# Inverting 16-token diagonal blocks on VectorE, with one doubling stage of two products, in a hybrid retention and gated-delta block

## The reference, cut to what matters

```python
kk = jnp.einsum("bhncd,bhnsd->bhncs", k, k)
lower = jnp.where(strict, beta[..., :, None] * kk * decay, 0.0)
a_mat = jnp.broadcast_to(eye, lower.shape) + lower
sol = lax.linalg.triangular_solve(a_mat, rhs, left_side=True, lower=True, unit_diagonal=True)
...
ret_out = ro * jax.nn.silu(rg)
...
gdn_out = go.reshape(b, t, GDN_W) * jax.nn.silu(gz)
```

## Time and profile before

| | |
|---|---|
| Time, median (lowest to highest) | 2764.13 us (2758.5 to 2767.09) |
| The profiled execution | 2768.09 us, span 2765.9 us |
| Granted TensorE clock | 0.993 |
| PE busy | 98% of the span |
| POOL, DVE, ACT busy | 60%, 53%, 38% |
| The chain that ended last | PE 86%, DVE 7%, issue 3%, POOL 2% |

### The profile page before, as it was taken

How to read it: one execution, slowest core, us unless ns; L and a number is a source line. 1 busy time by engine, 2 the same in 40 slices (tenths; PEclk the granted TensorE clock), 3 DMA queues, 4 the chain that set the end, 5 groups by cost and what they waited for, 6 DMA issues and landing times.

```text
span 2765.9 us, 36134 instructions
## 1 busy us (share of the span) xinstructions
PE 2702.6 (98%) x13344; PEld 2261.7 (82%) x13344; DVE 1462.1 (53%) x2423; ACT 1057.9 (38%) x1831; POOL 1647.1 (60%) x1260
## 2 busy tenths in 40 slices
PE   5899999999999999999999999999999999999998
PEld 4788888888888888888888888888888888888886
DVE  5867667454758475644456445663535553322223
ACT  3533333353334433443344424353333333443332
POOL 3745555576666755665566755576555566665653
PEclk9999999999999999999999999999999999999999
DMA  7334454332333223322232323422222224233242
GB/s 277 115 109 139 151 176 153 126 116 94 111 127 117 96 92 121 112 94 85 89 130 93 103 83 111 143 86 88 88 88 84 88 81 145 92 99 99 92 130 84
DMA packets 98238, 311.56 MB, mean 113 GB/s; under 512 B 11536, under 2 KB 11536, under 8 KB 95888
## 3 DMA queue, kind: packets, MB, share of 16 engines
q1 hardware_dynamic: 67248, 246.85, 27.1%
q10 hardware_dynamic: 30816, 62.40, 6.8%
HBM read 285.09 MB, written 24.12 MB: 112 GB/s over the span
## 4 chain that ended last, share of the span: by engine, by line
PE 86%; DVE 7%; issue 3%; POOL 2%; DMA 1%; ACT 1%; ACTq 0%; SPq 0%; DVEq 0%; POOLq 0%
PE acc L510 25%; PE acc L512 24%; PE acc L511 24%; PE pm L545 6%; PE pm L550 1%; DVE mixing L1242 1%; DVE x L1525 1%; PE pm L672 1%; PE pm L647 1%; DMA mixing<-in_ada_w 1%; POOL w L1693 1%; PE pm L600 1%; PE pm L642 1%; POOL mT L1702 1%; PE pm L657 0%
## 5 line engine op out<-in xcount | busy, mean ns | idle before, releaser
L1693 POOL TENSOR_TENSOR w<-raw,w 128x512 fp32r<-128x512 f32 x832 | 1117.7, 1345 | 938.6 <-ACT w L754 936.3
L754 ACT ACTIVATE w<-raw 128x512 fp32r<-128x512 f32 x832 | 520.9, 627 | 773.6 <-PE acc L512 722.7
L510 PE MATMUL acc<-mT,w 128*128 128x512 f32 x1536 | 623.3, 406 | 8.0 <-DVE mT L1587 3.2
L512 PE MATMUL acc<-mT,w 128*128 128x512 f32 x1536 | 601.9, 392 | 0.0
L511 PE MATMUL acc<-mT,w 128*128 128x512 f32 x1536 | 600.5, 391 | 0.0
L510 PE MATMUL acc<-hid,w 128*128 128x512 f32 x864 | 348.6, 404 | 2.2 <-DVE ffs L1485 1.4
L510 PEld LDWEIGHTS acc<-mT,w 128*128 128x128 f32 x1536 | 290.4, 189 | 67.2 <-issue 5.0
L512 PEld LDWEIGHTS acc<-mT,w 128*128 128x128 f32 x1536 | 289.5, 189 | 62.8
L512 PE MATMUL acc<-hid,w 128*128 128x512 f32 x864 | 337.4, 391 | 0.0
L511 PE MATMUL acc<-hid,w 128*128 128x512 f32 x864 | 336.8, 390 | 0.0
L511 PEld LDWEIGHTS acc<-mT,w 128*128 128x128 f32 x1536 | 290.8, 189 | 54.2 <-issue 1.0
(11 more groups left out here) (234 smaller groups left out, 3649.9 us busy)
## 6 DMA issues: line engine op xcount, KB each, us to landing
raw<-in_w_all SPq DMA_DIRECT2D x416, 512.0 KB, 3.5
ada_late<-in_ada_w SPq DMA_DIRECT2D x32, 512.0 KB, 5.5
xr<-in_xT ACTq DMA_DIRECT2D x48, 256.0 KB, 3.5
mixing<-in_ada_w SPq DMA_DIRECT2D x8, 1024.0 KB, 9.5
proj_kept<-ffs ACTq DMA_DIRECT2D x32, 256.0 KB, 2.1
out<-io ACTq DMA_DIRECT2D x32, 256.0 KB, 2.5
mixed_kept<-mixing ACTq DMA_DIRECT2D x28, 256.0 KB, 2.0
xr<-mixed_kept ACTq DMA_DIRECT2D x28, 256.0 KB, 2.7
```

What stands on the lines that cost most here:

```text
L510: e.matmul(bank, whi, x[:, 0, :], start=first, stop=False)
L512: m = e.matmul(bank, wlo, x[:, 0, :], start=False, stop=last)
L754: e.activation(w2[:, 0, local % HALVES, :], raw[:, tile % NRAW, local % 2 * NT:(local % 2 + 1) * NT], ACT.Copy).then_inc(S["w_hi"], 1)
L1693: e.tensor_tensor(w2[:, 1, local % HALVES, :], raw[:, tile % NRAW, local % 2 * NT:(local % 2 + 1) * NT], w2[:, 0, local % HALVES, :].bitca ...
```

## The change

The blocks that DVE inverts are 16 wide (OCT = 16). Its inversion has 15 steps of a product and a sum on 128x64 elements, in slots 20 to 27, two steps a slot. The running inverse `inv8` lies in the first 64 columns of PSUM bank bE, where it was in `octs`; `part8` and the rows stay in SBUF. There are 4 row buffers (ROWS): four shuffles follow `near`, and each of the first 11 steps ends with the shuffle of the row four further on. The expansion to `U` and the transpose to `T` are at s = 29.

Stage 0 now widens from 16 to 64 with its four products, at slots 32, 34, 36 and 38. After it `U` is updated by DVE, and the top left 64x64 part of each tile is transposed to `T` with three `transpose`s of 32 partitions by 4x32 elements. The last doubling, 64 to 128, is two products only, at slots 40 and 42, and one subtraction. So a unit has six `four`s for the inverse where it had eight. The masks for the stages change with the sizes; POOL's second one goes from s = 34 to 36. Both gate products are issued at s = 16, ahead of `r_state` and `LT` of s = 17.

```diff
-OCT = 8
+OCT = 16
+ROWS = 4
+YSTEPS = 4
...
-        near, inv8, part8 = (oct_cols(i) for i in range(3))
+        near, part8 = oct_cols(0), oct_cols(1)
+        inv8 = bE[:, 0:SUB * OCT].rearrange("p (t j) -> p t j", j=OCT)
 
         def near_row(i):
-            return oct_cols(3 + i)
+            return oct_cols(2 + i % ROWS)
+
+        def block_step(n, i):
+
+            return OSTEPS * n + 1 + ROWS + 2 * i + min(i, OCT - 1 - ROWS)
...
-                st, step = divmod(s - 30, 8)
-                if 0 <= st < STAGES and step == 0:
+                if s in (32, 40):
+                    st = (s - 32) // 8
                     e.wait_ge(S["lvl_mask"], STAGES * n + st + 1)
                     if st == 0:
                         e.wait_ge(S["k_nat"], n + 1)
                         e.wait_ge(S["t_ready"], n + 1)
                     else:
-                        e.wait_ge(S["t_next"], (STAGES - 1) * n + st)
+                        e.wait_ge(S["t_next"], 3 * (n + 1))
                     four(bE, Lm, T).then_inc(S["x_out"], 1)
-                if 0 <= st < STAGES and step == 2:
+                if s in (34, 42):
+                    st = (s - 34) // 8
                     e.wait_ge(S["x_ready"], STAGES * n + st + 1)
                     if st:
-                        e.wait_ge(S["u_turned"], (STAGES - 1) * n + st)
+                        e.wait_ge(S["u_half"], n + 1)
                     else:
                         e.wait_ge(S["u_first"], n + 1)
                         e.wait_ge(S["lt_ready"], n + 1)
                     four(bB, X, U).then_inc(S["y_out"], 1)
-                if 0 <= st < STAGES and step == 4:
-                    e.wait_ge(S["q_ready"], 2 * STAGES * n + 2 * st + 1)
+                if s == 36:
+                    e.wait_ge(S["q_ready"], 2 * n + 1)
                     four(bB, X, Q).then_inc(S["y_out"], 1)
-                if 0 <= st < STAGES and step == 6:
-                    e.wait_ge(S["q_ready"], 2 * STAGES * n + 2 * st + 2)
-                    if st == 0:
-                        e.wait_ge(S["attn_ready"], n + 1)
-                    if st < STAGES - 1:
-                        four(bF, Q, X).then_inc(S["y_out"], 1)
-                    else:
-                        four(bF, X, Q).then_inc(S["y_out"], 1)
+                if s == 38:
+                    e.wait_ge(S["q_ready"], 2 * n + 2)
+                    e.wait_ge(S["attn_ready"], n + 1)
+                    four(bF, X, Q).then_inc(S["y_out"], 1)
...
+                def row_of_block(i):
+
+                    e.stream_shuffle(octs[:, 2 + i % ROWS, :], octs[:, 0, :], [OCT * (q // OCT) + i for q in range(32)]).then_inc(
+                        S["oct_steps"], 1)
...
-                if s == 26:
+                if s == 16:
                     twice_silu(S["tanh_rg"], n, gts[:, 0, :], gts[:, 0, :], pr[:, RG - RK, :], S["y_rg"])
-                if s == 28:
+                if s == 16:
                     twice_silu(S["tanh_gz"], n, gts[:, 1, :], gts[:, 1, :], pr[:, GZ - RK, :], S["y_gz"])
...
-                    for i in range(OCT - 1):
-                        e.stream_shuffle(octs[:, 3 + i, :], octs[:, 0, :], [OCT * (q // OCT) + i for q in range(32)]).then_inc(
-                            S["oct_steps"], 1)
-                for i in {20: (0, 1), 21: (2, 3), 22: (4, 5), 23: (6,)}.get(s, ()):
-                    done = OSTEPS * n + OCT + 2 * i
+                    for i in range(ROWS):
+                        row_of_block(i)
+                for i in (2 * (s - 20), 2 * (s - 20) + 1):
+                    if not (20 <= s < 28 and i < OCT - 1):
+                        continue
                     if n == 0 and i == 0:
                         e.wait_ge(S["eye8_ready"], 1)
+                    if i == 0:
+                        e.wait_ge(S["k_nat"], n + 1)
                     before = inv8 if i else eye8.unsqueeze(1).to_broadcast([P, SUB, OCT])
-                    e.wait_ge(S["oct_steps"], done)
+                    e.wait_ge(S["oct_steps"], block_step(n, i - 1) + 2 if i else block_step(n, 0))
                     e.tensor_tensor(part8, near_row(i), before[:, :, i:i + 1].to_broadcast([P, SUB, OCT]),
                                     ALU.mult).then_inc(S["oct_steps"], 1)
-                    e.wait_ge(S["oct_steps"], done + 1)
+                    e.wait_ge(S["oct_steps"], block_step(n, i) + 1)
                     e.tensor_tensor(inv8, before, part8, ALU.add).then_inc(S["oct_steps"], 1)
-                if s == 25:
+                    if i + ROWS < OCT - 1:
+                        row_of_block(i + ROWS)
+                if s == 29:
                     e.wait_ge(S["oct_steps"], OSTEPS * (n + 1))
                     e.tensor_tensor(by_oct(U), inv8.unsqueeze(2).to_broadcast([P, SUB, P // OCT, OCT]),
                                     lmask[:, 1, :].rearrange("p (b j) -> p b j", j=OCT).unsqueeze(1).to_broadcast(
                                         [P, SUB, P // OCT, OCT]), ALU.mult).then_inc(S["u_first"], 1)
                     e.wait_ge(S["u_first"], n + 1)
                     e.transpose(T, U).then_inc(S["t_ready"], 1)
-                st, step = divmod(s - 30, 8)
-                if 0 <= st < STAGES and step in (2, 4):
-                    e.wait_ge(S["y_out"], 3 * STAGES * n + 3 * st + step // 2)
-                    if st:
-                        e.wait_ge(S["u_turned"], (STAGES - 1) * n + st)
+                if s in (34, 36):
+                    at = (s - 34) // 2
+                    e.wait_ge(S["y_out"], YSTEPS * n + at + 1)
+                    e.wait_ge(S["u_first"], n + 1)
+                    if at == 0:
+                        e.wait_ge(S["mg_kept"], 16 * ((HEADS - 1) * (n // HEADS) + n % HEADS))
                     else:
-                        e.wait_ge(S["u_first"], n + 1)
-                    if st == 0 and step == 2:
-                        e.wait_ge(S["mg_kept"], 16 * ((HEADS - 1) * (n // HEADS) + n % HEADS))
+                        e.wait_ge(S["q_ready"], 2 * n + 1)
                     e.tensor_tensor(Q, U, bB, ALU.subtract).then_inc(S["q_ready"], 1)
-                if 0 <= st < STAGES and step == 6:
-                    e.wait_ge(S["y_out"], 3 * STAGES * n + 3 * st + 3)
-                    if st < STAGES - 1:
-                        if st:
-                            e.wait_ge(S["t_next"], (STAGES - 1) * n + st)
-                        else:
-                            e.wait_ge(S["t_ready"], n + 1)
-                        e.tensor_tensor(T, T, bF, ALU.subtract).then_inc(S["t_next"], 1)
-                        e.wait_ge(S["t_next"], (STAGES - 1) * n + st + 1)
-                        e.transpose(U, T).then_inc(S["u_turned"], 1)
-                    else:
-                        e.wait_ge(S["u_turned"], (STAGES - 1) * (n + 1))
-                        e.tensor_tensor(U, U, bF, ALU.subtract).then_inc(S["u_next"], 1)
+                if s == 38:
+                    e.wait_ge(S["y_out"], YSTEPS * n + 3)
+                    e.wait_ge(S["q_ready"], 2 * n + 2)
+                    e.wait_ge(S["t_ready"], n + 1)
+                    e.tensor_tensor(U, U, bF, ALU.subtract).then_inc(S["u_half"], 1)
+                    e.wait_ge(S["u_half"], n + 1)
+                    for i, j in ((0, 0), (1, 1), (0, 1)):
+                        e.transpose(by_sub(T)[32 * j:32 * j + 32, :, 32 * i:32 * i + 32],
+                                    by_sub(U)[32 * i:32 * i + 32, :, 32 * j:32 * j + 32]).then_inc(S["t_next"], 1)
+                if s == 42:
+                    e.wait_ge(S["y_out"], YSTEPS * n + 4)
+                    e.wait_ge(S["t_next"], 3 * (n + 1))
+                    e.tensor_tensor(U, U, bB, ALU.subtract).then_inc(S["u_next"], 1)
```

More of the change, by code:

```diff
@@ L228 @@
 hf_ready h_hi h_lo h0_even h0_odd x0_ready
-own_steps u_turned nq_ready oct_masked oct_steps eye8_ready
+own_steps nq_ready oct_masked oct_steps eye8_ready
 wg_split gate_rows gate_copied gate_out gate_steps gate_exp
@@ L236 @@
 gt_out sqk_ready sqq_ready ss_steps nk_ready k_nat v_nat q_ready
-kk_out attn_ready lt_ready lvl_mask u_first t_ready x_out x_ready y_out t_next u_next
+kk_out attn_ready lt_ready lvl_mask u_first t_ready x_out x_ready y_out t_next u_half u_next
 negc_ready gvar silu_v mod_steps gates_done ks_out r_ready tr_out vnew_ready upd_out g_state o2_out
@@ L293, in build @@
         lmask = sb("lmask", [P, 2 + STAGES, P])
-        octs = sb("octs", [P, 3 + OCT - 1, SUB * OCT])
+        octs = sb("octs", [P, 2 + ROWS, SUB * OCT])
         para = sb("para", [P, HEADS, PAR])
@@ L323, in build @@
         gbt = small[:, 192:208]
-        eye8 = small[:, 248:256]
+        eye8 = small[:, 48:64]
         vnorm, nk2, bnk = (small[:, 216 + 4 * i:220 + 4 * i] for i in range(3))
@@ L933, in front @@
                     e.wait_ge(S["conv_steps"], 12 * m + 8)
-                    e.wait_ge(S["y_out"], 3 * STAGES * m)
+                    e.wait_ge(S["y_out"], YSTEPS * m)
```

(29 more changed lines are left out.)

## The result

| | before | after |
|---|---|---|
| Time, median (lowest to highest) | 2764.6 us (2758.5 to 2767.1) | 2738.8 us (2736.1 to 2742.6) |
| Ratio, 95% interval | | 0.9911 (0.989 to 0.9932) |
| The profiled execution | span 2765.9 us | span 2738.6 us |
| PE busy, idle | 2702.6, 63.3 us | 2671.2, 67.4 us |
| DVE busy | 1462.1 us | 1461.7 us |

The changed kernel is faster by 25.8 us in the medians and by 27.3 us in the spans; the forecast was 2739 us, a span of 2740.6.

What follows compares the result with a forecast made beforehand. The prediction took PE's number of matmuls as the bound. Its terms, -28.5 - 0.8 + 4.0 = -25.3 us, took the span from 2765.9 to 2740.6 and the median to 2739 us, range 2728 to 2750.

Steps and rivals of the forecast that it cites:

- What bounds the kernel: Whole run: the number of matmuls PE must issue sets the end; PE work removed shortens the run equally unless PE waits.
- 28.5 us of PE work: PE's inverse products: 32 `four`s removed over 16 units at 0.89 us each, all on the path.
- The 0.8 us wait of `r_cross`: PE's only wait on DVE's retention state, once, 0.8 us: it goes.
- The chain on DVE: 15 block inversion steps: 9.3 us plus 1.0 for PSUM, 10.3 in all; T ready 14.4 us after `near` starts.
- 0.07 for PSUM: Each block step on DVE: the sum takes 0.07 us more for writing PSUM, the product 0; 1.0 us over 15 steps.
- 0.14 us of its own: Shuffles in 11 of the 15 block steps on DVE: each adds 0.14 us with 64 elements.
- 4 us of wait at slots 32 of units 0 to 3: PE waits for T at slot 32, 1.0 us in each of four early units, 4 in all, 0 to 8.
- DVE loses two subtractions and a transpose; nothing comes of it: DVE's work per unit: two subtractions and a full transpose fewer, priced at nothing because DVE isn't the bound.
- B: Units 0 to 3 wait longer at slot 32, about 2.9 us each: 2746 us, within 2743 to 2752; chance 0.18.
- C: PE's saving comes back as waits for weights or free banks: 2752 to 2768, say 2760 us; chance 0.07.
- D: DVE's chain operations held up as before, 1.1 us a step: slower, 2765 to 2800, middle 2782 us; chance 0.05.

Runs made afterwards that it cites:

- the kernel with the other parts alone: Kernel before, blocks of 8 and eight products a unit, with only the running inverse in PSUM and the gate products at slot 16: 2763.5 us, ratio 1.0002.
- the changed kernel's second profile: The changed kernel, nothing altered, measured once more on one chip with later variants: 2737.4 us, ratio 0.9908.
- seven steps: Changed kernel with steps 7 to 14 of the block inversion left out, so blocks are not fully inverted: 2737.7 us, ratio 0.9913.

## Why the prediction was right

**What bounds the kernel: right.** PE's list of matmuls does. Two products put back take the whole gain away, and 57 us of DVE work taken out change nothing.

**28.5 us of PE work: right in size.** Doubled products cost 26.1 us of busy time, 2.4 less than forecast. Between before and after it is 31.4 us. Part of the difference is the clock: the mean granted clock is 0.994 where it was 0.993, and the stretches at half speed add up to 27.3 us in before's profile and to 20.5 in both of the changed kernel's, 3.4 us of full-speed time less. Some 2 us are in neither. PE runs at 1.2 GHz in place of 2.4 in a few short stretches early in the run. The same two windows, 120 to 160 and 450 to 520 us, in before and then in after (the granted clock is the number behind POOL's count):

```profile
120.00:160.00 40.00, 34.16 (x174) 28.68 (x173) 27.75 (x57) 13.46 (x26) 24.40 (x19) 0.90 0.39 125
450.00:520.00 70.00, 70.00 (x344) 59.47 (x345) 34.46 (x52) 25.51 (x47) 38.99 (x28) 0.91 0.45 146
```

```profile
120.00:160.00 40.00, 35.86 (x181) 30.85 (x182) 30.94 (x92) 13.77 (x26) 24.51 (x20) 0.91 0.40 132
450.00:520.00 70.00, 69.87 (x347) 59.62 (x348) 33.78 (x51) 28.32 (x52) 42.82 (x32) 0.93 0.43 139
```

By these rounded means, 40 x 0.10 + 70 x 0.09 = 10.3 us are lost there in before and 3.6 + 4.9 = 8.5 in after. The kernel before ran at 0.992 to 0.996 from one execution to the next, so this part is no property of the change.

**The 0.8 us wait of `r_cross`: right.** It is gone in after and in the kernel with the other parts alone.

**The chain on DVE: mechanism right, size wrong.** Forecast was a step of 0.69 us (0.62 and 0.07 for PSUM), measured 0.53. Two terms were mis-sized. The sum was given 0.07 us for writing to PSUM. It has a mean of 232 ns with a maximum of 233, and the sum with everything in SBUF has a median of 225 (the kernel with the inverse in SBUF): 0.01 us, not 0.07. The forecast had its 0.07 from a comparison of unlike rows. The taps of rows 8 take their factor from a column with one value for each partition (`cw`), the operation of rows 6 has the constant 1.0 in its place. Like beside like, in before, a tap with everything in SBUF, and an operation that reads PSUM with a constant:

```profile
L1242 DVE SCALAR_TENSOR_TENSOR mixing<-pg,para,mixing x36: 743/752/1803, 79.6 to 1505.9; 128x512 f32<-128x512 f32 x36
```

```profile
L1485 DVE SCALAR_TENSOR_TENSOR ffs<-acc,ffr x128: 676/691/694, 600.7 to 2707.3; 128x512 f32<-128x512 f32 x128
```

The tap has a median of 752 ns without any PSUM, and the other, with it, 691. So in these operations the 0.07 us go with the factor by partition and not with PSUM, and where the prediction says that the trace agrees with the Trainium skill for the taps, it doesn't bear that out. And the shuffle was given 0.14 us of its own in 11 steps. It starts 0.15 us after the sum, needs nothing from it, and the next product starts 0.28 after the sum against 0.27 without a shuffle: it lies in time that the product must wait anyway. Together 1.0 + 1.5 us: T came 11.8 us after `near`, not 14.4.

**4 us of wait at slots 32 of units 0 to 3: wrong, it is 0.** This follows from the chain; the margin was 1.7 us, not -0.9. The gate products' place decides over it: back in slots 26 and 28 the wait appears, 2.9 us.

**"DVE loses two subtractions and a transpose; nothing comes of it": wrong.** The sum had no term for what PE meets behind the removed products. PE's idle time rose by 4.1 us (by 2.4 in the changed kernel's second profile). In units 0 to 2 PE waits 0.5 us at slot 47 for the first residual. PE and DVE meet at slot 42, where the last subtraction starts as the product ends; unit 1 of after:

```profile
258.52 1.05 PE L552 MATMUL pm<-mixing 128*128 128x128 f32 x8
```

```profile
259.61 0.69 DVE L1390 TENSOR_TENSOR mixing<-mixing,pm 128x512 f32<-128x512 f32 x1
```

From there to slot 47 PE's list has lost a product (slot 44, 0.9 us) and DVE's a subtraction (0.6 us from start to start), and the rotation is still in it. This is argued from the rows. Shown is that what PE has to do ahead of slot 42 doesn't enter: with two products more at slots 36 and 38 the three waits are the same, and PE is idle for 65.9 us, as in the second profile of the changed kernel (65.7). So most of the 2.4 us seem to come with the new order of the lists, whether PE has six products or eight; the other 1.7 of the 4.1 are mainly a single wait of 2.4 us in unit 3 (450.13), which the second profile doesn't have. In both profiles, and in the kernel with eight products too, PE waits some 3 us longer for the norm's rows (L533, L527) than in before; no run tells why. Where the two products are taken out of the kernel before and DVE's list stays, the idle time rises by 8.4 us.

The rise is about what was forecast for slot 32, so the total was met with the wait in the wrong place: -28.5 - 0.8 (forecast) + 4.1 + 0.8 (the idle time's rise, with the lost wait counted back) - 2.9 (the rest of the busy time, mostly clock) = -27.3 us of span. The agreement to the microsecond is in part luck.

**The rivals.** B: no wait at slot 32 or 40. C: one wait for the weights, 0.5 us. D: its mechanism is real, and in the kernel that has it the time is 2779 us, forecast 2782; the mean of L1365 was the right row to rule it out. Its places, the early units and late dense results, were right too, but not its sizes: a step is 0.53 + 0.43 = 0.96 us there, not 1.1, units 0 to 3 wait 11.0 us more where the forecast had 25, and 12.0 us are longer busy time, mostly clock, for which it had no term. That the totals agree is luck as well.

## What to carry to other kernels

When PE's own list sets the end, price a removed matmul by start distances, not by record lengths, and then look for the next place at which PE meets another engine: the slots right behind the removed work are where the gain leaks, and moving one instruction of that engine's list behind the one that PE waits for can get it back (4.6 us here for one slot). An operand's place can be worth nothing alone and decide whether a change built on it gains 25 us or loses 16. Before a row is used as the price of a memory, check that the two operations compared differ in nothing else. A margin of a chain is measured on the longest run of work that shares its engine; what stands in the middle of it, as the state update here, waits first.

## What the runs showed of the hardware

- DVE, two-operand operations on 128x64 fp32: 211 to 213 ns with one input in PSUM and the output in SBUF, 232 with input and output in PSUM, and medians of 217 (product) and 225 (sum) with everything in SBUF. With both inputs in SBUF and POOL at work, single ones last up to 1365 ns and the mean is 421 to 458.
- DVE, three-operand operations on 128x512 fp32: 680 ns in SBUF and 691 with an input in PSUM where the factor is a constant, 752 in SBUF and 747 to 756 with PSUM where it is a column with a value for each partition (medians, in before). An extra of 0.07 us for PSUM shows in none of them. It is otherwise for the first tap, which has one tensor and one column (L1239 of before): a median of 486 ns with its output in SBUF and of 748 with it in PSUM.
- PE, fp32 products of 128x128 by 128: 0.82 to 0.89 us for four in a row. With 64 moved columns the same, with 64x64 operands 0.79, including the cost of going over from and back to the 128-wide matmuls.
- PE's mean granted clock was 0.991 in the run with 92.4 us of idle time and 0.993 to 0.995 in all the others, with 60 to 72 us and in no order by it: 0.993 with 63.3 (before), 0.995 with 68.3 (seven steps). Which of its waits make the clock fall wasn't tested.
